# Query and key projections with a head's weights as the stationary operand, and rotary embedding on features

## What is computed

```python
z, xbc, dt_raw, q, k, v = jnp.split(h @ w_in[l], split_at, axis=-1)
y_ssd = ssd_mixer(z, xbc, dt_raw, ...)
y_diff = diff_attention(q, k, v, cos, sin, lam, ...)

def apply_rope(x, cos, sin):          # x: (B, L, heads, 2, 64)
    x1, x2 = jnp.split(x, 2, axis=-1)
    rot = jnp.concatenate([-x2, x1], axis=-1)
    return x * cos + rot * sin
```

## Time and profile before

| | us |
|---|---|
| median of three executions | 1446.27 |
| the profiled execution | 1446.21 |
| its span, first to last instruction | 1444.5 |
| TensorE busy (matmul) | 1418.7 |
| TensorE busy (weight load) | 1187.2 |
| VectorE busy | 932.4 |
| ScalarE busy | 662.5 |
| GpSimd busy | 65.7 |

### The profile page before, as it was taken

The page is one execution under the profiler, slowest core; times in us unless marked ns, Lnnn a source line. Parts: engine busy times, 40 slices in busy tenths (PEclk is TensorE's granted clock), DMA queues, the critical chain, the costliest instruction groups (busy, mean ns, idle before and its releaser), DMA issues.

```text
span 1444.5 us, 19634 instructions
## 1 busy us (share of the span) xinstructions
PE 1418.7 (98%) x7272; PEld 1187.2 (82%) x7280; DVE 932.4 (65%) x1543; ACT 662.5 (46%) x1298; POOL 65.7 (5%) x116
## 2 busy tenths in 40 slices
PE   9999999999998999999999999999999999999998
PEld 7889888886668988888888888888888888888886
DVE  4883565728877624642653788887665585467898
ACT  6324222327776523532532675444445464454443
POOL 1000000000001101110000300000000000000011
PEclk9999999999999999999999999999999999999999
DMA  9212111102003622310231343664333797766463
GB/s 322 60 33 59 30 30 30 37 23 88 1 1 103 206 101 88 117 59 29 77 112 60 129 127 123 235 208 170 141 145 131 268 353 258 249 226 197 148 233 130
DMA packets 94606, 185.52 MB, mean 128 GB/s; under 512 B 10160, under 2 KB 28592, under 8 KB 92464
## 3 DMA queue, kind: packets, MB, share of 16 engines
q1 hardware_dynamic: 87312, 153.30, 31.4%
q10 hardware_dynamic: 7200, 30.97, 6.3%
HBM read 142.30 MB, written 41.94 MB: 128 GB/s over the span
## 4 chain that ended last, share of the span: by engine, by line
PE 86%; DVE 4%; ACT 3%; issue 3%; DMA 2%; SPq 1%; POOL 0%; ACTq 0%; DVEq 0%; POOLq 0%
PE ps L2184 26%; PE ps L2186 26%; PE ps L2185 26%; PE ps L2385 1%; PE ps L2326 1%; ACT probs L1002 1%; DMA x_in<-in_x_dram 1%; PE ps L2424 1%; PE ps L2243 1%; PE ps L2404 1%; DVE nmax L1656 1%; DVE wl L1383 1%; PE ps L2344 1%; PE ps L2329 1%; ACT junk L842 0%
## 5 line engine op out<-in xcount | busy, mean ns | idle before, releaser
L2184 PE MATMUL ps<-wh,oph 128*128 128x512 f32 (+1 forms) x576 | 214.9, 373 | 0.0
L2186 PE MATMUL ps<-wh,opl 128*128 128x512 f32 (+1 forms) x576 | 211.0, 366 | 0.0
L2185 PE MATMUL ps<-wl,oph 128*128 128x512 f32 (+1 forms) x576 | 210.3, 365 | 0.0
L2184 PE MATMUL ps<-d_ring 128*128 128x512 f32 x448 | 174.3, 389 | 0.0
L2186 PE MATMUL ps<-d_ring 128*128 128x512 f32 x448 | 174.3, 389 | 0.0
L2185 PE MATMUL ps<-d_ring 128*128 128x512 f32 x448 | 174.3, 389 | 0.0
L2186 PEld LDWEIGHTS ps<-wh,opl 128*128 128x128 f32 x576 | 108.1, 188 | 18.0
L2184 PEld LDWEIGHTS ps<-wh,oph 128*128 128x128 f32 x576 | 108.2, 188 | 16.8 <-issue 0.2
L2185 PEld LDWEIGHTS ps<-wl,oph 128*128 128x128 f32 x576 | 108.4, 188 | 16.5
L791 POOL TENSOR_TENSOR rms<-stat,mhalf 128x1 f32<-128x1 f32 (+2 forms) x59 | 55.6, 944 | 1344.8 <-DVE stat L1387 1323.2
L1303 ACT ACTIVATE d_ring<-left_raw 128x512 fp32r<-128x512 f32 x112 | 70.2, 627 | 95.1 <-PE ps L2186 75.8
(11 more groups left out here) (359 smaller groups left out, 2871.7 us busy)
## 6 DMA issues: line engine op xcount, KB each, us to landing
right_raw<-in_w_down_dram SPq DMA_DIRECT2D x128, 256.0 KB, 4.1
u_kept_s<-us SPq DMA_DIRECT2D x64, 256.0 KB, 2.5
left_raw<-u_kept_s SPq DMA_DIRECT2D x64, 256.0 KB, 2.9
w_blk<-in_w_up_blocks_dram ACTq DMA_DIRECT2D x14, 1024.0 KB, 5.6
left_raw<-u_kept_a SPq DMA_DIRECT2D x48, 256.0 KB, 3.1
raw<-in_w_in_dram SPq DMA_DIRECT2D x16, 512.0 KB, 3.9
u_kept_a<-u SPq DMA_DIRECT2D x24, 256.0 KB, 2.2
x_in<-in_x_dram SPq DMA_DIRECT2D x8, 512.0 KB, 9.4
```

Source lines behind the costliest of these rows:

```text
L2184: te.matmul(o, lh, rh, start=first, stop=False, skip_group_check=more)
L2185: te.matmul(o, lh, rl, start=False, stop=False, skip_group_check=more)
L2186: return te.matmul(o, ll, rh, start=False, stop=last, skip_group_check=more)
```

## The change

For q and k, `wide_step` now takes 128 weight columns (one head) as the stationary operand and 512 tokens as the moving one, so that features lie on partitions at once. The tile number i of `QKZ_STEPS` now means head i % 4 and token half i // 4. The number of matmuls and their columns are the same. The four transposes per tile and the last two rounds of TensorE's loop are gone.

At the n where a tile is finished, ScalarE copies it out of PSUM into its place in `qt` or `kt` (`rope_raw`), waits for that copy, and issues four DMAs that copy four groups of 32 partitions x 512 columns (64 KB each) to `rope_rot0` or `rope_rot1` with neighbouring groups exchanged. From the third tile on, ScalarE first waits until VectorE has finished the tile two before, since that one's buffer is used again; the very last tile waits for the one just before, because `rope_rot0` lies in its place. `rope_raw` stands ahead of `ssd_act` in the order of one n. VectorE's `rope` now runs two steps later, waits for the four DMAs, and does three operations of 128 x 512, all in SBUF: two multiplications and an addition.

The tables are now 128 x 1024, for one feature per partition and all tokens. The positions come as a broadcast row of 1024 integers on every partition (512 KB, one DMA on ScalarE's queue after the normaliser rows). The frequency and the sign of each partition are picked out with the identity matrix. VectorE computes the angles in four parts at n = 1, 2, 3 and 4 of the v steps, ScalarE makes the two tables at n = 5 (one Abs and two Sin over 1024 columns), and VectorE scales both at n = 8. Some small buffers move.

```diff
-        rope_t = at("rope_t", "K", 64, [P, 3, NT, HALF_DIM])
+        rope_rot = [at("rope_rot0", "K", 14336, [P, 512]), at("rope_rot1", "TMP", 2048, [P, 512])]
...
-        y_off = at("y_off", "TMP", 2048, [P, 512])
-        roped = at("roped", "TMP", 4096, [P, 2, 512])
-        rope_b = at("rope_b", "MISC", 5376, [P, 512])
+        y_off = at("y_off", "TMP", 10240, [P, 512])
...
-        cos_t = at("cos_t", "MISC", 0, [P, NT, HALF_DIM])
-        sin_t = at("sin_t", "MISC", 1024, [P, NT, HALF_DIM])
-        nsin_t = at("nsin_t", "MISC", 2048, [P, NT, HALF_DIM])
-        dts = [at(f"dts{n}", "MISC", 3072 + 256 * n, [P, NT, SSD_H]) for n in range(9)]
+        cos_t = at("cos_t", "TMP", 4096, [P, T])
+        sin_t = at("sin_t", "MISC", 0, [P, T])
+        pos_i = at("pos_i", "MISC", 0, [P, T], I32)
+        inv_d = at("inv_d", "TMP", 4096, [P, 4, HALF_DIM])
+        dts = [at(f"dts{n}", "MISC", 5120 + 256 * n, [P, NT, SSD_H]) for n in range(9)]
...
-            act.dma_start(pos_i[:], t["positions_t"]).then_inc(rows_loaded, 16)
...
-            act.wait_ge(rope_r, 1)
-            act.wait_ge(consts_ready, ALL_CONSTS)
-            s.activation(sin_t[:], rope_t[:, 0], ACT.Sin).then_inc(rope_sin, 1)
-            s.activation(nsin_t[:], rope_t[:, 0], ACT.Sin, scale=-1.0).then_inc(rope_sin, 1)
-            after(s.activation(rope_t[:, 1], rope_t[:, 0], ACT.Abs))
-            s.activation(cos_t[:], rope_t[:, 1], ACT.Sin, scale=-1.0, bias=half_pi[:]).then_inc(rope_sin, 1)
+            act.dma_start(pos_i[:], rows(t["positions"][0:1, :])).then_inc(rows_loaded, 16)
+
+            def rope_tables():
+
+                act.wait_ge(rope_r, 1)
+                act.wait_ge(consts_ready, ALL_CONSTS)
+                after(s.activation(cos_t[:], sin_t[:], ACT.Abs))
+                s.activation(sin_t[:], sin_t[:], ACT.Sin).then_inc(rope_sin, 1)
+                s.activation(cos_t[:], cos_t[:], ACT.Sin, scale=-1.0, bias=half_pi[:]).then_inc(rope_sin, 1)
...
-            def rope_evac(name, i, n):
-
-                act.wait_ge(rt_done, n + 1)
-                s.activation((qt if name == "q" else kt)[:, :, i * P:(i + 1) * P],
-                             ps[:, 3, :].rearrange("p (k c) -> p k c", k=4), ACT.Copy,
-                             scale=0.125 if name == "q" else 1.0).then_inc(rt_ev, 1)
+            def rope_raw(name, i, n, g):
+
+                place = (qt if name == "q" else kt)[:, i % 4, i // 4 * 512:(i // 4 + 1) * 512]
+                act.wait_ge(pj_done, g + 1)
+                if n == 0:
+                    act.wait_ge(dt_v, 4)
+                    act.wait_ge(rms_seen, 2)
+                if n >= 2:
+                    act.wait_ge(rt_ev, n if (name, i) == ("k", NT - 1) else n - 1)
+                s.activation(place, ps[:, bank(g), :], ACT.Copy, scale=0.125 if name == "q" else 1.0).then_inc(ev[name], 1)
+                act.wait_ge(ev[name], n % NT + 1)
+                for a in range(4):
+                    b = a ^ 1
+                    act.dma_start(rope_rot[n % 2][32 * a:32 * a + 32, :], place[32 * b:32 * b + 32, :]).then_inc(rot_loaded[n % 2], 16)
...
+                if n in ROPE_AT:
+                    rope_raw(*ROPE_AT[n], g)
+                if n == 5:
+                    rope_tables()
...
-                if n - 2 in ROPE_AT:
-                    rope_evac(*ROPE_AT[n - 2])
...
-            ang, turns = rope_t[:, 0], rope_t[:, 2]
-            after(v.tensor_tensor(ang, pos_f[:].unsqueeze(2).to_broadcast([P, NT, HALF_DIM]),
-                                  inv[:].unsqueeze(1).to_broadcast([P, NT, HALF_DIM]), ALU.mult))
-            after(v.tensor_scalar(turns, ang, 1.0 / (2 * math.pi), None, ALU.mult))
-            after(v.tensor_scalar(turns, turns, ROUND, None, ALU.add))
-            after(v.tensor_scalar(turns, turns, -ROUND, None, ALU.add))
-            for part in (TWO_PI_A, TWO_PI_B, TWO_PI_C):
-                after(v.scalar_tensor_tensor(ang, turns, -part, ang, ALU.mult, ALU.add))
-            v.tensor_scalar(ang, ang, PI_SAFE, -PI_SAFE, ALU.min, ALU.max).then_inc(rope_r, 1)
+            after(v.tensor_tensor(inv_d[:], ident[:].rearrange("p (a c) -> p a c", a=4),
+                                  inv[:].unsqueeze(1).to_broadcast([P, 4, HALF_DIM]), ALU.mult))
+            first = inv_d[:].rearrange("p (a h) c -> p a h c", h=2)[:, :, 0, :]
+            after(v.tensor_scalar(first, first, -1.0, None, ALU.mult))
+            after(v.tensor_reduce(inv_c[:], inv_d[:].rearrange("p a c -> p (a c)"), AX.X, ALU.add))
+
+            def rope_angles(part):
+
+                ang, turns = sin_t[:], cos_t[:]
+                if part == 0:
+                    dve.wait_ge(rows_loaded, 32)
+                    after(v.tensor_copy(turns, pos_i[:]))
+                    after(v.tensor_scalar(ang, turns, inv_c[:], None, ALU.mult))
+                elif part == 1:
+                    after(v.tensor_scalar(turns, ang, 1.0 / (2 * math.pi), None, ALU.mult))
+                    after(v.tensor_scalar(turns, turns, ROUND, None, ALU.add))
+                    after(v.tensor_scalar(turns, turns, -ROUND, None, ALU.add))
+                elif part == 2:
+                    for piece in (TWO_PI_A, TWO_PI_B, TWO_PI_C):
+                        after(v.scalar_tensor_tensor(ang, turns, -piece, ang, ALU.mult, ALU.add))
+                else:
+                    v.tensor_scalar(ang, ang, PI_SAFE, -PI_SAFE, ALU.min, ALU.max).then_inc(rope_r, 1)
+
+            def rope_scale():
+
+                dve.wait_ge(rope_sin, 2)
+                for table in (sin_t, cos_t):
+                    v.tensor_tensor(table[:], table[:], rms_b[:], ALU.mult).then_inc(rms_seen, 1)
...
-            dve.wait_ge(rope_sin, 3)
-            for table in (cos_t, sin_t, nsin_t):
-                v.tensor_tensor(table[:], table[:], rms[:, 0:NT].unsqueeze(2).to_broadcast([P, NT, HALF_DIM]), ALU.mult).then_inc(rms_seen, 1)
...
-            def rope(name, i, n, g):
-
-                dve.wait_ge(pj_done, g + 1)
+            def rope(name, i, n):
+
+                cut = slice(i // 4 * 512, (i // 4 + 1) * 512)
+                place, rot = (qt if name == "q" else kt)[:, i % 4, cut], rope_rot[n % 2][:]
                 if n == 0:
-                    dve.wait_ge(rms_seen, 3)
-                if n >= 2:
-                    dve.wait_ge(rt_done, n - 1)
-                src = ps[:, bank(g), :].rearrange("p (a h c) -> p a h c", a=8, h=2)
-                dst = roped[:, n % 2, :].rearrange("p (a h c) -> p a h c", a=8, h=2)
-                tmp = rope_b[:].rearrange("p (a h c) -> p a h c", a=8, h=2)
-                spread_t = lambda tab: tab[:, i, :].unsqueeze(1).to_broadcast([P, 8, HALF_DIM])
-                for h in range(2):
-                    v.tensor_tensor(dst[:, :, h, :], src[:, :, h, :], spread_t(cos_t), ALU.mult)
-                if n:
-                    dve.wait_ge(rope_done, n)
-                v.tensor_tensor(tmp[:, :, 0, :], src[:, :, 1, :], spread_t(nsin_t), ALU.mult)
-                v.tensor_tensor(tmp[:, :, 1, :], src[:, :, 0, :], spread_t(sin_t), ALU.mult).then_inc(ev[name], 1)
-                dve.wait_ge(ev[name], i + 1)
-                v.tensor_tensor(roped[:, n % 2, :], roped[:, n % 2, :], rope_b[:], ALU.add).then_inc(rope_done, 1)
+                    dve.wait_ge(rms_seen, 2)
+                dve.wait_ge(rot_loaded[n % 2], 64 * (n // 2 + 1))
+                v.tensor_tensor(rot, rot, sin_t[:, cut], ALU.mult).then_inc(dv, 1)
+                v.tensor_tensor(place, place, cos_t[:, cut], ALU.mult).then_inc(dv, 1)
+                n_dv[0] += 2
+                dve.wait_ge(dv, n_dv[0])
+                v.tensor_tensor(place, place, rot, ALU.add).then_inc(rt_ev, 1)
...
-                if n in ROPE_AT:
-                    rope(*ROPE_AT[n], STEP0["v"] + n)
+                if n - 2 in ROPE_AT:
+                    rope(*ROPE_AT[n - 2])
...
+                if 1 <= n < 5:
+                    rope_angles(n - 1)
...
+                if n == 8:
+                    rope_scale()
...
+                    if name in ("q", "k"):
+                        f, cut = tile % 4 * P, slice(tile // 4 * 512, (tile // 4 + 1) * 512)
+                        ins = three(ps[:, bank(g), :], wcols(wh, slot, k, f, P, 512), wcols(wl, slot, k, f, P, 512),
+                                    lh[:, kk, cut], ll[:, kk, cut], fresh and k == 0, not fresh and k == 3)
+                        continue
...
-            def rope_transpose(n):
-
-                pe.wait_ge(rope_done, n + 1)
-                if n:
-                    pe.wait_ge(rt_ev, n)
-                for b in range(4):
-                    ins = te.transpose(ps[:, 3, b * P:(b + 1) * P], roped[:, n % 2, b * P:(b + 1) * P], ident[:])
-                ins.then_inc(rt_done, 1)
-
-            for n in range(66):
-                if n < 64:
-                    name, st = STEPS[STEP0["v"] + n]
-                    if name == "v":
-                        token_step(name, st, oph, opl, st % NT)
-                    else:
```

(29 more changed lines are left out.)

## The result

Six executions of the changed kernel, beside six of the kernel before on the same chip:

| | before | after |
|---|---|---|
| median, us | 1446.80 | 1453.01 |
| lowest to highest, us | 1446.14 to 1447.95 | 1451.49 to 1455.23 |
| profiled execution, us | 1446.21 | 1451.49 |
| its span, us | 1444.5 | 1449.8 |
| mean granted TensorE clock | 0.999 | 0.994 |

The account below looks back on a forecast made before the run. TensorE, busy 124.6 of 125 us, was taken as the bound, with the order of waits deciding what is free. -8.1 + 0.3 + 2.5 + 4.4 = -0.9 us gave 1445.3 us, range 1441.5 to 1450.0.

Parts of the forecast that it names:

- The matmul's price: TensorE's z steps: matmuls of old and new form both start 0.224 us apart, a step of 12 taking 2.7 us.
- What goes: TensorE's 64 transposes in 16 groups, with late matmuls and waits behind them: 8.1 us off the path.
- The ten groups that stand alone: Transpose groups not following the scan's products: the 0.1 us late start of the matmul behind each goes, 1.0 us.
- the six behind the scan's products: Transpose groups following the scan's products: the 0.1 us late start of the next matmul stays.
- ScalarE's four DMAs: Issuing four DMA instructions per tile on ScalarE: between 1.36 and 1.78 us, taken as 1.55.
- Landing: Arrival of a tile's last DMA: taken as 2.5 us, from a transfer out of SBUF in a quiet stretch.
- Place A: Wait for k's unit 1 at n = 35: VectorE ready at 15.6 us, TensorE at 13.1, stall 2.5 us.
- Place B: Chunk 7's outputs at n = 50: VectorE ready at 12.6 us, TensorE at 8.2, stall 4.4 us.
- The v steps: Wider angle tables delay the step sizes in the v steps: between 0 and 0.8 us, taken as 0.3.
- Rival 1: Waits at A and B shorter than counted: 4 us faster, 1442.3 us, or 1438.4 without any stall; chance 0.27.
- Rival 2: DMAs land late, past the 4.4 us hidden, 3 us per 1 us of landing: up to 1451.0 us; chance 0.13.
- Rival 3: Clock falls in stall B, one or two steps 2.7 us longer each: 1448.0 to 1450.7 us; chance 0.10.

Follow-up runs that it names:

- other order: Against the changed kernel, VectorE's low parts of both weight halves precede tile 7's rotary, ScalarE's high parts its copy and exchange: 1448.08 us.

## Why the prediction was wrong

Point by point, in its own steps:

- **The matmul's price**, 0.224 us in the new form too: held. The distance is 0.23 wherever the clock is full.
- **What goes**, 8.1 us: the right term, 0.9 us too small. The stretch without stalls is 9.0 us shorter, 0.565 us for each of the 16 groups. The ten groups that stand alone were charged rightly: five cost 0.45 us each, five with a wait 0.76, together 6.0. What was short is the six behind the scan's products. The prediction let the late start of the next matmul "stay" there, 0.35 us a group; in fact the second matmul behind the products comes 0.44 us sooner without the group (behind chunk 2's last products 177.74 to 178.84 before, 177.05 to 177.71 after). That is 0.5 of the 0.9 us; where the rest went is open.
- **ScalarE's four DMAs**, taken at 1.55 us: the term that was mis-sized. 2.44 us, and 2.96 at A. Its bounds, 1.36 and 1.78, did not reach it: both came from loads out of memory, and no row had a copy between parts of the on-chip memory. Landing, taken at 2.5, was 2.0 (once 4.5).
- **Place A**: forecast 15.6 us from the end of chunk 3's outputs, measured 16.8 (208.16, which is 0.39 ahead of VectorE's last part, to 224.95). VectorE's tile 5 rotary ended at 5.8 (5.85 forecast), ScalarE's split at 10.6 (9.25): 1.4 later by the four DMAs, and the rest as forecast. TensorE arrived at 13.1, as forecast. Stall 3.65 instead of 2.5.
- **Place B**: forecast 12.6 from the start of step 48, measured 292.52 - 278.79 = 13.7. First part and rotary ended at 4.3 (4.1), DMAs at 7.5 (6.4), decays at 10.3 (8.9), and the middle part's product 3.4 us later (3.7). TensorE arrived at 8.2, as forecast. Stall 5.5 instead of 4.4. The mechanism was right link by link, and a third buffer, which cuts the link that was named, takes it away.
- **The v steps**, taken at 0.3: nothing. VectorE's clip ended at 118.24 instead of 119.4, as single-input operations on 1024 columns took 0.69 to 0.75 us and not 0.82, and no table load stood before the sines. VectorE has the step sizes by 129.6, before at 129.8. The clip on its timeline:

```profile
117.55 0.69 DVE L1467 TENSOR_SCALAR sin_t<-sin_t 128x1024 f32<-128x1024 f32 x1
```

- **Rival 1**, shorter waits: fell; they were longer.
- **Rival 2**, late landings: fell; VectorE waited 0.9 us for them in 16 tiles, and most landed in less than half of the 4.4 us that were allowed.
- **Rival 3**, the clock falls in stall B: this is what happened, and at A too. It had a chance of 0.10, and its price of 2.7 to 5.4 us for B alone is met by 3.8. **The step that failed is the one that kept the clock at full rate behind the stalls.** The argument was that 1.6 us without work leave it at 1.00 and that no longer gap stood in the trace. That is no evidence for gaps of 2.5 and 4.4 us: a row covers what it shows, and both forecast gaps lay outside it. The sum had named two such gaps itself, and counted the clock's fall as somebody else's case instead of as a term of each. The rule of the Trainium skill, "TensorE: Matmul & The Clock Gate", section "Why this matters for your kernels", quoted against the change, was right, and the trace agrees with it: 0.50 of full clock behind gaps of 3.5 and 5.4 us.

The sum with what was measured: -9.0 + 0 + 3.65 + 1.8 + 5.5 + 3.8 = +5.75 us, and the stretch grew by 236.77 - 231.04 = 5.73. By size, the clock makes 5.6 of the error of 6.6 us in the stretch (forecast -0.9, measured +5.7), the longer stalls, nearly all of it the DMAs' issue, 2.3, the transposes -0.9 and the v steps -0.3.

## What to carry to other kernels

A stall that a change creates on a TensorE at full clock can have two prices, its length and the matmuls behind it at half the clock; where the sum of a change forecasts a gap longer than any that the trace shows at full clock, the fall belongs in the sum. An engine's mean room says nothing about a handover: here ScalarE was busy 37 of 125 us before the change, and 2.4 us of DMA issuing on it still cost TensorE at two places, so issues belong on a queue that nothing waits behind. Where a wait protects a buffer, look whether a third buffer is free before the change is judged: 2 KB per partition turned 9.3 us of loss at one place into 0.6 in the profiled execution, and took 6.5 us off the median.

## What the runs showed of the hardware that was not expected

- Issuing an on-chip copy of 32 partitions costs ScalarE's queue 0.51 us for the first of a row and 0.61 for each that follows (SyncE 0.51 and 0.59), and one of 128 partitions with four times the bytes 0.49. The longest row of four took 3.48 us (the version "other order", 215 to 218 us, while weights were loaded).
- The clock fell behind gaps of 2.4, 3.1, 3.5, 3.6, 5.4 and 5.5 us, and not behind 1.0 and 1.4 us in the same stage. The price of a fall does not follow the gap: at A it was 1.8 us and 2.85 us behind gaps of 3.5 and 3.6 us, at B 3.4 us behind 2.4, 1.8 behind 3.1 and 3.8 behind 5.4, each in one profiled execution with the same work behind the gap.
- Matmuls that nothing reads keep the clock up at no cost in a gap that is there anyway: 37 of them made the kernel 5.8 us faster.
- At the attention's end the clock falls in some executions of a kernel and not in others, at the same waits; it costs 1.5 to 1.8 us and is part of the spread of up to 4 us between the executions of a kernel.
